# The first MLP's down projection by seven products of half tiles instead of eight

## The reference

```python
def squared_relu_mlp(x, w1, w2):
    return jnp.square(jax.nn.relu(x @ w1)) @ w2
...
f = squared_relu_mlp(rms_norm(h, pre_mlp_norm[i]), w_mlp_in[i], w_mlp_out[i])
h = h + rms_norm(f, post_mlp_norm[i])
```

## Time and profile before

| | us |
|---|---|
| median of 3 runs (lowest, highest) | 2288.51 (2285.66, 2289.23) |
| span of the profiled execution, first to last instruction | 2286.1 |
| TensorE busy | 2252.4 |
| VectorE busy | 1267.0 |
| ScalarE busy | 657.5 |
| GpSimd busy | 1577.5 |
| first MLP's up and down stages in the trace, about | 336 to 687 |

### The profile page before, as it was taken

The page is one execution under the profiler, slowest core; times in us unless marked ns, Lnnn a source line. Parts: engine busy times, 40 slices in busy tenths (PEclk is TensorE's granted clock), DMA queues, the critical chain, the costliest instruction groups (busy, mean ns, idle before and its releaser), DMA issues.

```text
span 2286.1 us, 27986 instructions
## 1 busy us (share of the span) xinstructions
PE 2252.4 (99%) x10594; PEld 1848.7 (81%) x10594; DVE 1267.0 (55%) x1852; ACT 657.5 (29%) x1201; POOL 1577.5 (69%) x1534
## 2 busy tenths in 40 slices
PE   8999999999999999999999999999999999999998
PEld 6888888888888788888888888888677788888887
DVE  7774746335345777175554364368865445626354
ACT  3443432101013455154221011142464233202113
POOL 8666568777777455644597777779445938878784
PEclk9999999999999999999999999999999999999999
DMA  5222233333333111211243333324222413333332
GB/s 168 87 73 85 70 92 92 102 100 98 96 97 89 55 39 40 76 42 53 78 118 108 97 108 104 97 84 142 82 65 70 124 52 97 97 98 97 97 95 77
DMA packets 114264, 202.35 MB, mean 89 GB/s; under 512 B 13009, under 2 KB 21713, under 8 KB 114129
## 3 DMA queue, kind: packets, MB, share of 16 engines
q1 hardware_dynamic: 109424, 194.67, 29.3%
q10 hardware_dynamic: 4704, 5.89, 0.8%
HBM read 196.19 MB, written 2.10 MB: 87 GB/s over the span
## 4 chain that ended last, share of the span: by engine, by line
PE 89%; DVE 5%; POOL 3%; ACT 2%; issue 0%; DMA 0%; SPq 0%; DVEq 0%; POOLq 0%; ACTq 0%
PE bank L499 26%; PE bank L501 26%; PE bank L500 26%; POOL wL L2907 2%; DVE bank L2025 1%; DVE h L2017 1%; PE bank L966 1%; POOL wH L2905 1%; PE bank L548 1%; PE bank L936 1%; PE bank L935 1%; PE bank L937 1%; PE bank L673 1%; PE bank L943 1%; PE bank L944 1%; DVE aL L2025 1%
## 5 line engine op out<-in xcount | busy, mean ns | idle before, releaser
L2907 POOL TENSOR_TENSOR wL<-raw,wH 128x512 fp32r<-128x512 f32 (+2 forms) x732 | 1012.2, 1383 | 61.0
L2905 POOL TENSOR_SCALAR wH<-raw 128x512 fp32r<-128x512 f32 (+2 forms) x732 | 525.9, 718 | 533.1 <-PE bank L501 459.0
L499 PE MATMUL bank<-aH,wH 128*128 128x512 f32 (+2 forms) x1392 | 548.5, 394 | 8.4 <-DVE aL L2025 7.3
L501 PE MATMUL bank<-aH,wL 128*128 128x512 f32 (+2 forms) x1392 | 539.7, 388 | 0.0
L500 PE MATMUL bank<-aL,wH 128*128 128x512 f32 (+2 forms) x1392 | 539.5, 388 | 0.0
L499 PE MATMUL bank<-uH,wH 128*128 128x512 f32 (+1 forms) x1010 | 384.1, 380 | 0.0
L500 PE MATMUL bank<-uL,wH 128*128 128x512 f32 (+1 forms) x1010 | 382.4, 379 | 0.0
L501 PE MATMUL bank<-uH,wL 128*128 128x512 f32 (+1 forms) x1010 | 382.4, 379 | 0.0
L499 PEld LDWEIGHTS bank<-aH,wH 128*128 128x128 f32 (+1 forms) x1392 | 261.8, 188 | 67.5 <-POOL wL L2907 7.2
L500 PEld LDWEIGHTS bank<-aL,wH 128*128 128x128 f32 (+1 forms) x1392 | 261.9, 188 | 55.3 <-issue 3.2
L501 PEld LDWEIGHTS bank<-aH,wL 128*128 128x128 f32 (+1 forms) x1392 | 261.6, 188 | 54.3
(11 more groups left out here) (325 smaller groups left out, 3177.3 us busy)
## 6 DMA issues: line engine op xcount, KB each, us to landing
raw<-in_ws SPq DMA_DIRECT2D x698, 256.0 KB, 2.6
raw<-in_ws SPq DMA_DIRECT2D x24, 192.0 KB, 2.3
d_xr<-F ACTq DMA_DIRECT2D x32, 67.5 KB, 2.8
h<-in_xT SPq DMA_DIRECT2D x8, 256.0 KB, 5.7
E<-in_memT ACTq DMA_DIRECT2D x16, 128.0 KB, 2.7
raw<-in_ws SPq DMA_DIRECT2D x10, 128.0 KB, 2.1
tmp<-in_pT ACTq DMA_DIRECT2D x4, 256.0 KB, 3.2
out<-c_F SPq DMA_DIRECT2D x2, 512.0 KB, 2.8
```

The source lines that it names most:

```text
L499: P.e.matmul(o, lH, rH, start=start, stop=False, skip_group_check=skip)
L501: return P.e.matmul(o, lL, rH, start=False, stop=stop, skip_group_check=skip)
L2905: G.e.tensor_scalar(H, x, 1.0, 0.0, MUL, ADD).then_inc(*G.did("wH", n))
L2907: G.e.tensor_tensor(L, x, H.bitcast(F32), SUB).then_inc(*G.did("w", n))
```

## The change

In layer 0 the 8 x 8 tiles (k, output) of a group's weights and its 8 k tiles of activations are taken in two-by-two blocks: two output tiles (m = 0 to 3), k tiles even and odd (four pairs p), tokens in two halves of 256. Each block product is made by seven products of sums, in Winograd's form of Strassen's method, in place of eight. For block (g, m) TensorE makes the products in the order a11, s1, s2, a12, s3, s4, a22, each 4 pairs x 3 matmuls of 256 columns. They share partial results by accumulating onto each other: after a11, ACT copies R1 to R2, where s2 is added; after s2, it copies R2 to the upper half of R34, where s3 is added; after s3, from there to the lower half, where a22 is added.

- Weights: four raw pieces a11, a21, a12, a22 make seven factors, which fill the ring of seven. DVE makes the sums s1 = a21 + a22, s2 = s1 + a11, s4 = s2 + a12 in two PSUM banks and their low parts; GpSimd makes s3 = a11 + a21 and the low parts of a11, a12, s3, a22; ACT makes all seven high parts. The factors of block m + 1 are made while block m runs, those of block 0 at the last up tiles.
- Activations: seven combinations of the halves of a pair of tiles. ACT squares both tiles into Q, DVE makes the three differences, ACT copies high parts, DVE makes the low parts.
- PSUM: six banks belong to the block (two for sums, R1, R2, R34, R5) from the end of the ups of g = 0 on; two are left for the up tiles. A bank of an up tile comes free after ACT's square, no longer after DVE's relu.
- Results are added to `F` by DVE, in g = 0 in part by ACT; in g = 3 the odd tile of each block is turned in sign. The last tile's halves end in other order.
- The first MLP's tiles `uH`, `uL` become one array `u` of the same size, with `u2` of 12 more tiles. `PLAN` stays the list of loads; a second list, `SLOTS`, is the list of ring slots. Layer 1 is as before.

The core of the diff (eight columns of indentation taken off; the rest changes indices from `PLAN` to `SLOTS`, memory, and the same order of calls in ACT's list as in DVE's):

```diff
+FACTORS = ("a11", "s1", "s2", "a12", "s3", "s4", "a22")
+COMBO = {"a11": 0, "s1": 1, "s2": 5, "a12": 2, "s3": 4, "s4": 3, "a22": 6}
+RAW = {"a11": 0, "a21": 1, "a12": 2, "a22": 3}
...
+    def seven(name, layer, g, m):
+at = len(out)
+for odd, c in ((0, 0), (0, 1), (1, 0), (1, 1)):
+    out.append((name, layer, tuple(8 * g + 2 * p + odd for p in range(4)), cols((128 * (2 * m + c), 128))))
+for factor in FACTORS:
+    slots.append((factor, at))
     def tile8(name, layer, c0, ks=k8):
 add(name, layer, ks, cols((c0, 128)))
...
+        for m in range(4):
+            seven("w_mlp_out", layer, g, m)
+    else:
+        down("w_mlp_out", layer, tuple(range(8 * g, 8 * g + 8)), g == 0)
 embed(layer, 1)
 open3(*[("w_ple_gate", layer, 128 * o) for o in range(3)])
...
+def c_scratch(Q, gi):
+    flat = Q[:, :, :].rearrange("p a t -> p (a t)")
+    return (Q[:, 0:2, 0:256], Q[:, 3, :].rearrange("p (a t) -> p a t", a=2),
+            flat[:, 768:1536].rearrange("p (a t) -> p a t", a=3))[gi]
+def slot(n, kind):
+    return {"s1": bk("sum7", 0), "s2": bk("sum7", 1), "s4": bk("sum7", 0)}[kind][:, :] if kind in ("s1", "s2", "s4") else \
+        s3sum[:, :] if kind == "s3" else raw[(SLOTS[n][1] + RAW[kind]) % NR][:, :]
...
+    def seven(i, g, m, ready):
+        nonlocal at
+        key = (i, g, m)
+        R1, R2, R34, R5 = (bk(n)[:, :] for n in ("R1", "R2", "R34", "R5"))
+        into = {"a11": R1[:, 0:256], "s1": R5[:, 0:256], "s2": R2[:, 0:256], "a12": R1[:, 0:256],
+                "s3": R34[:, 256:512], "s4": R2[:, 0:256], "a22": R34[:, 0:256]}
+        for kind in FACTORS:
+            n, o, c = at, into[kind], COMBO[kind]
+            assert n == slot_of(i, g, m, kind)
+            at += 1
+            H, L = (w[n % NW][:, :].rearrange("p (k c) -> p k c", k=4) for w in (wH, wL))
+            P.wait_ge(V if kind in ("s1", "s2", "s4") else G, "w", n)
+            if kind in ("a11", "s1") and (g or m):
+                P.wait_ge(A if before(i, g, m)[1] == 0 else V, "R1" if kind == "a11" else "R5", *before(i, g, m))
+            if kind in ("s2", "a12"):
+                P.wait_ge(A, "U1", *key)
+            if kind in ("s3", "s4"):
+                P.wait_ge(A, "U2", *key)
+            if kind == "a22":
+                P.wait_ge(A, "U3", *key)
+            for p in range(4):
+                ready(p, c)
+                x = combo(p, c)
+                first = kind in ("a11", "s1") and p == 0
+                P.e.matmul(o, L[:, p, :], x[:, 0:256], start=first, stop=False, skip_group_check=True)
+                P.e.matmul(o, H[:, p, :], x[:, 0:256], start=False, stop=False, skip_group_check=True)
+                j = P.e.matmul(o, H[:, p, :], x[:, 256:512], start=False, stop=p == 3, skip_group_check=True)
+            j.then_inc(*P.did(kind, *key))
+            P.also("w", n)
     def mlp_ple(i, keys_next, events_next):
         def p_ready(k):
             P.wait_ge(A, "pH", i, held["j"], k)
...
+                if i == 0 and g == 0 and o == 6:
+                    own += [take("sum7", 0), take("sum7", 1)]
...
             P.also("up done", i, g)
+            if i == 0:
+                if g == 0:
+                    own += [take(n) for n in ("R1", "R5", "R2", "R34")]
+                for m in range(4):
+                    seven(i, g, m, lambda p, c: P.wait_ge(V, "cL", g, p, (0, 0, 1, 1, 2, 2, 2)[c]))
+                P.also("down done", i, g)
+                if g == 3:
...
+    def factor_high(i, g, m, *kinds):
+        for kind in kinds:
+            n = slot_of(i, g, m, kind)
+            r = SLOTS[n][1]
+            if kind in ("s1", "s2", "s4"):
+                A.wait_ge(V, "s", slot_of(i, g, m, "s2" if kind == "s1" else "s4"))
+            elif kind == "s3":
+                A.wait_ge(G, "s3", n)
+            else:
+                A.wait_ge(raw_in[(r + RAW[kind]) % NR], r + RAW[kind])
+            A.wait_ge(P, "w", n - NW)
+            do(wH[n % NW][:, :], slot(n, kind), ACT.Copy).then_inc(*A.did("wH", n))
+    def up_seven(g, o):
+        Q, p = mlp_Q[0], o // 2
+        A.wait_ge(V, "r", 0, g, o)
+        if g or p:
+            A.wait_ge(V, "cL", *((g, p - 1) if p else (g - 1, 3)), 1)
+        do(Q[:, 3 if o % 2 else 0, :], bk("up", 0, g, o)[:, :], ACT.Square).then_inc(*A.did("sqr", g, o))
+        if g and o < 2:
+            A.wait_ge(P, "down done", 0, g - 1)
+        for gi in (1, 2) if o % 2 else (0,):
+            if gi == 1:
+                A.wait_ge(A, "sqr", g, o)
+            else:
+                A.wait_ge(V, "t5" if gi == 0 else "t4", g, p)
+            a, b = C_GROUPS[gi]
+            do(combos(p, a, b)[:, :, 0:256], c_scratch(Q, gi), ACT.Copy).then_inc(*A.did("cH", g, p, gi))
+    def down_seven(i, g, m):
+        key = (i, g, m)
+        R1, R2, R34, R5 = (bk(n)[:, :] for n in ("R1", "R2", "R34", "R5"))
+        F0, F1, lo, hi = F[:, 2 * m, :], F[:, 2 * m + 1, :], half_cols(0), half_cols(1)
+        A.wait_ge(P, "a11", *key)
+        if g or m:
+            A.wait_ge(V, "R2", *before(*key))
+        do(R2[:, lo], R1[:, lo], ACT.Copy).then_inc(*A.did("U1", *key))
+        if m < 3:
+            factor_high(i, g, m + 1, "a11", "s1")
+        if g == 0:
+            A.wait_ge(P, "s1", *key)
+            do(F[:, 2 * m:2 * m + 2, hi], R5[:, lo].unsqueeze(1).to_broadcast([128, 2, 256]), ACT.Copy).then_inc(
+                *A.did("R5", *key))
+        A.wait_ge(P, "s2", *key)
+        if g or m:
+            A.wait_ge(V, "R34", *before(*key))
+        do(R34[:, hi], R2[:, lo], ACT.Copy).then_inc(*A.did("U2", *key))
+        if m < 3:
+            factor_high(i, g, m + 1, "s2", "a12")
+        A.wait_ge(P, "s3", *key)
+        do(R34[:, lo], R34[:, hi], ACT.Copy).then_inc(*A.did("U3", *key))
+        if g == 0:
+            do(F0[:, lo], R1[:, lo], ACT.Copy).then_inc(*A.did("R1", *key))
+        if m < 3:
+            factor_high(i, g, m + 1, "s3", "s4", "a22")
     def mlp_ple(i, next_pre):
-        mr, E = mlp_r[i], mlp_E[i]
+        Q, E = mlp_Q[i], mlp_E[i]
+        mr = [Q[:, 1, :], Q[:, 2, :]]
         def embedded(*tiles):
             for o in tiles:
...
+    def factor_sums(i, g, m, *steps):
+        n1, n2, n4 = (slot_of(i, g, m, kind) for kind in ("s1", "s2", "s4"))
+        r = SLOTS[n1][1]
+        S0, S1 = bk("sum7", 0)[:, :], bk("sum7", 1)[:, :]
+        def part(kind):
+            V.wait_ge(raw_in[(r + RAW[kind]) % NR], r + RAW[kind])
+            return raw[(r + RAW[kind]) % NR][:, :]
+        for step in steps:
+            if step == "s1":
+                if g or m:
+                    V.wait_ge(V, "w", slot_of(*before(i, g, m), "s4"))
+                a21, a22 = part("a21"), part("a22")
+                tt(S0, a21, a22, ADD).then_inc(*V.did("s", n1))
+            elif step == "s2":
+                a11 = part("a11")
+                V.wait_ge(V, "s", n1)
+                tt(S1, S0, a11, ADD).then_inc(*V.did("s", n2))
+            elif step == "s4":
+                a12 = part("a12")
+                V.wait_ge(V, "s", n2)
+                V.wait_ge(V, "w", n1)
+                tt(S0, S1, a12, ADD).then_inc(*V.did("s", n4))
+            else:
+                n = {"l1": n1, "l2": n2, "l4": n4}[step]
+                V.wait_ge(A, "wH", n)
+                low(wL[n % NW][:, :], S1 if step == "l2" else S0, wH[n % NW][:, :]).then_inc(*V.did("w", n))
+    def combo_low(g, p, gi):
+        a, b = C_GROUPS[gi]
+        V.wait_ge(A, "cH", g, p, gi)
+        low(combos(p, a, b)[:, :, 256:512], c_scratch(mlp_Q[0], gi), combos(p, a, b)[:, :, 0:256]).then_inc(
+            *V.did("cL", g, p, gi))
+    def up_seven(g, o):
+        Q, p = mlp_Q[0], o // 2
+        V.wait_ge(P, "up", 0, g, o)
+        x = bk("up", 0, g, o)[:, :]
+        stt(x, x, 0.0, root("x", 0), ALU.max, MUL).then_inc(*V.did("r", 0, g, o))
+        V.wait_ge(A, "sqr", g, o)
+        if o % 2 == 0:
+            tt(Q[:, 1, 0:256], Q[:, 0, 0:256], Q[:, 0, 256:512], SUB).then_inc(*V.did("t5", g, p))
+            combo_low(g, p, 0)
+        else:
+            tt(Q[:, 1, 256:512], Q[:, 3, 256:512], Q[:, 0, 256:512], SUB)
+            stt(Q[:, 2, 0:256], Q[:, 1, 0:256], -1.0, Q[:, 3, 256:512], MUL, SUB).then_inc(*V.did("t6", g, p))
+            V.wait_ge(V, "t6", g, p)
+            stt(Q[:, 2, 256:512], Q[:, 2, 0:256], -1.0, Q[:, 3, 0:256], MUL, SUB).then_inc(*V.did("t4", g, p))
+            combo_low(g, p, 2)
+            combo_low(g, p, 1)
+    def down_seven(i, g, m):
+        key = (i, g, m)
+        R1, R2, R34, R5 = (bk(n)[:, :] for n in ("R1", "R2", "R34", "R5"))
+        F0, F1, lo, hi = F[:, 2 * m, :], F[:, 2 * m + 1, :], half_cols(0), half_cols(1)
+        both = F[:, 2 * m:2 * m + 2, hi]
+        if m < 3:
+            factor_sums(i, g, m + 1, "s1", "s2", "l1")
+        if g:
+            V.wait_ge(P, "s1", *key)
+            tt(both, both, R5[:, lo].unsqueeze(1).to_broadcast([128, 2, 256]), ADD).then_inc(*V.did("R5", *key))
+        if m < 3:
+            factor_sums(i, g, m + 1, "s4", "l2")
+        if g:
```

(95 more changed lines are left out.)

119 lines of the change are left out of this document (92 added, 27 removed).

## The result

The changed kernel takes 2370.92 us (median of 4, 2369.13 to 2373.93) beside 2288.87 of the kernel before (4 runs, 2285.66 to 2289.76): ratio 1.0361, 95% interval 1.0347 to 1.0376. The prediction, 2364 in a range of 2330 to 2398 and slower, holds; the sum is 7 us short.

A forecast was written before the change was run, and what follows sets the result against it. TensorE, busy 99% of the span, was taken to bound the kernel. Matmuls -13.4, first blocks +66.5, blocks 1 and 2 +17, clock +5 make +75 us on 2288.5: 2364 us, range 2330 to 2398.

The forecast's parts named there:

- TensorE's saving: Down projection of the first MLP: seven products of half matmuls take 161.0 us in place of 174.4, 13.4 saved.
- First blocks: First block of each group: waits for DVE's and ACT's late up-stage work, 9.5 to 26 us each, 66.5 in all.
- The ring: Blocks 1 and 2 of each group: a22's slot, load, sums and copies form a loop; 2.1 us each, 17 in all.
- Clock: Waiting blocks: TensorE's idle time brings half speed at times, 5 us, bounds 0 and 25.
- The rest "within 1 us": The end's three half instructions in line and the squares in g = 3: within 1 us.
- hidden after all: Rival: in the up stages DVE's chain fits within TensorE's time, only the matmul saving is left; 2275 us, 4%.
- the one with clock and contention: Rival: the clock falls in each waiting block, +25 in place of 5, port contention at its upper half, +12; 2396 us, 14%.
- contention: Up stages: DVE waits for GpSimd at the shared SBUF port, 0.6 us per even tile, 1.1 per odd one.
- no ring: Rival: the raw of a22 is there early enough, so blocks 1 and 2 run at 10.06 us; 2338 us, 15%.

The follow-up runs named there:

- The run that cuts the ring: Against the changed kernel, the raw blocks of a22 get two buffers of their own, so their load no longer waits for a slot: 2343.66 us.
- The last run: Seven products in groups 1 and 2 alone, next group's up tiles ahead of blocks; against that kernel, raw a22 loaded before raw a12: 2283.28 us, 0.9977 of the kernel before.

## Why the prediction was right

- **TensorE's saving**: 13.4 forecast, 14.4 by the blocks without a wait (10.00 and not 10.06 us).
- **First blocks**: 66.5 forecast. Measured 27.0, 15.3, 13.2, 7.7 over 10.0, and 1.6 in the ups: 64.8, of which 3.8 is half clock behind the last wait, so 61.0 of waits. DVE's tiles in g = 3 began 5.7, 11.1, 18.5, 22.2, 28.4, 34.0, 41.7 and 45.8 us after the stage before (5.5 to 33.7, 42.7 and 47.8 forecast): tile 7 two us early, the last pairs being shorter than forecast. (An odd tile of 5.1 and 1.1 is 6.2 and not the 6.3 of the prediction, which changes nothing.) In g = 0 the last of the chain was at 401.2 and the block's end at 419.3 (401.8 and 418.4), but the wait before a11 was not named: I had TensorE wait from s1 on. That cost nothing, for in the run with 52 extra matmuls a11 began 6.0 us later and the block ended 1.2 us later.
- **The ring**: s3 at 7.64 us (7.6). Without the half clock the eight blocks lost 18.3 us (17). The run that cuts the ring shows the cause, and the run with group 0 plain shows that a group's losses are its own.
- **Clock**: the mis-sized term, 5 us taken within bounds of 0 and 25. Time from the last wait of a block to its end, less 1.43 us a product, is 9.7 us in blocks 1 and 2, 3.8 in the first blocks, 1.4 in block 3: 14.8. I had the reason only half: that slow work "is itself followed by a wait" holds in a first block, where the 26 and the 52 extra matmuls brought nothing; but in blocks 1 and 2 the wait ahead of s3 is the last, and nothing behind it hides the slow products. How much it is depends on the execution: of the eight waits before s3 in blocks 1 and 2, half rate came behind six in this profile, but behind four and three in those with 26 and 52 extra matmuls, where these blocks have the same code. So 14.8 is the size of this one execution, whose time was 2372.4 us, 1.4 over the median. The Trainium skill (TensorE: Matmul & The Clock Gate, What's actually happening) has the gate follow how busy the engine has been; the trace agrees, 1.00 in the up-stage windows and 0.50 to 0.83 in the windows of g = 0 above.
- **The rest "within 1 us"**: the squares of g = 3 cost 3.7 us of waiting in block 3; moving them took 4.0 off that block and put 0.2 to 1.4 on the one before. ACT's list there was not followed: the same kind of wait (a copy behind work that waits for DVE) that the other terms were made of.
- Sum: -14.4 + 61.0 + 18.3 + 3.7 + 14.8 = 83.4 us in the stage where 75 were forecast; the mechanism of each large term came as forecast, and the 5.5 us too many in the first blocks made up for a part of what the clock and the squares had too few. The rivals: "hidden after all" did not come; of the one with clock and contention, 14.8 us of half clock came where it has 25, and no more contention than forecast, as tile 7 shows; "no ring" is what the run with the ring cut made of it, 2343.7 where 2338 was given.
- That DVE was two thirds busy and still late was right; that a place for its lag can be found was not considered. The last run shows it: in groups 1 and 2 the chain is hidden by 10.9 us of the next group's matmuls.

## What to carry to other kernels

A wait on a result that passes between two engines in strict order is not shown by either's busy share: follow the chain through the in-order lists, queue of loads included, and give TensorE other work where the chain ends. Fewer multiplications pay only when every block runs without a gap; start them where cover exists, and leave the plain form where it doesn't. Cost the clock of a short wait by what comes behind it: the products behind the last wait may run slow and uncovered, those ahead of another wait are free. Don't read a single run's difference of a few us as an edit's: look for the block that changed, and for the same block in the other runs.
